# Score tiles kept in PSUM, a router on unnormalised tokens, and earlier expert panels in a two-layer float32 transformer kernel

## What is computed

```python
# layer 1 (x: 256 x 1024)
z = rms_norm(x) @ w_in                 # q, c_kv, q_idx, k_idx, w_idx, g_attn, x_rnn, g_rnn, merge
s_idx = sum_j relu(q_idx[j] @ layer_norm(k_idx).T) * w_idx[j]      # 8 index heads
keep  = top 64 keys of each token by s_idx, causal
o     = softmax(q_lat[h] @ c_kv.T - slope[h] * dist, over keep) @ c_kv   # 16 heads
y_a   = (o @ w_uv * silu(g_attn)) @ w_attn_proj
u     = causal_depthwise_conv(x_rnn)   # 4 taps
a     = exp(-8 * sigmoid(u @ w_a) * softplus(-lam))
h     = scan(h = a * h + sqrt(1 - a*a) * sigmoid(u @ w_x) * u)
x1    = x + (g_a * y_a + g_r * ((h * silu(g_rnn)) @ w_rnn_proj)) @ w_out
# layer 2: 8 MoBA heads and 8 MLA heads, gated and projected, then
x2    = rms(x1) + mixed2 @ w_out_2
hf    = rms_norm(x2)                   # ffn_norm gain
group = argmax(hf @ w_rg); the two best of its 8 experts by hf @ w_re   # 32 experts, width 256
out   = rms_norm(x2 + sum of weight * down(silu(hf @ gate) * (hf @ up)))
```

## Time and profile before

| | |
|---|---|
| median of 3 runs | 746.95 us (746.90 to 748.19) |
| the profiled execution | 748.94 us, span 747.1 us |
| PE busy | 666.2 us (89%) |
| DVE, ACT, POOL busy | 388.1, 333.6, 392.8 us |
| HBM read | 179.71 MB |
| transfer rate, 40 slices of 18.7 us | 421 GB/s in slices 27 and 28, 264 in slice 29, 415 to 423 in slices 30 to 39; 89 to 206 GB/s in slices 3 to 25 |
| mean granted clock of PE | 0.978 |

### The profile page before, as it was taken

One profiled execution on the slowest core, in us unless ns is written; L12 is line 12 of the kernel. 1 busy time (PEld: TensorE's weight loads), 2 busy tenths in 40 slices (PEclk: granted clock), 3 DMA queues, 4 the chain that ended last, 5 costly groups with the idle time before them and its releaser, 6 DMA issues.

```text
span 747.1 us, 13776 instructions
## 1 busy us (share of the span) xinstructions
PE 666.2 (89%) x5578; PEld 554.3 (74%) x5578; DVE 388.1 (52%) x664; ACT 333.6 (45%) x611; POOL 392.8 (53%) x284
## 2 busy tenths in 40 slices
PE   2999989989999999989999999998899997777754
PEld 2999879879989999988879998995654543343321
DVE  5899963599995247976855554624311110010002
ACT  7456657855653457554358665342212111111102
POOL 3789647687879989797798556970000000000000
PEclk9899999999999999999999999999999999999997
DMA  9735323433434554543454333799799999999992
GB/s 323 289 125 206 123 89 139 150 132 121 162 121 169 188 201 169 170 144 139 148 191 169 114 114 131 308 421 421 264 423 418 421 421 421 422 420 422 421 415 81
DMA packets 26129, 181.68 MB, mean 243 GB/s; under 512 B 2896, under 2 KB 3152, under 8 KB 4688
## 3 DMA queue, kind: packets, MB, share of 16 engines
q1 hardware_dynamic: 26064, 180.77, 63.2%
HBM read 179.71 MB, written 1.05 MB: 242 GB/s over the span
## 4 chain that ended last, share of the span: by engine, by line
PE 56%; DVE 19%; DMA 12%; issue 4%; ACT 4%; POOL 2%; SPq 2%; ACTq 0%; DVEq 0%
PE D L449 30%; PE L L880 5%; DVE big L1401 4%; DMA xT<-w_expert_dram 4%; DMA hT<-w_expert_dram 4%; DMA big<-w_expert_dram 4%; PE L L860 3%; PE QB L910 3%; DVE small L1401 2%; POOL ring_r L1384 2%; PE D L489 2%; PE D L917 2%; PE L L606 1%; SPq L388 1%; DVE big_r L1420 1%
## 5 line engine op out<-in xcount | busy, mean ns | idle before, releaser
L1384 POOL TENSOR_TENSOR ring_r<-ring,ring_r 128x512 fp32r<-128x512 f32 x280 | 392.6, 1437 | 108.6 <-ACT ring_r L1000 108.5
L449 PE MATMUL D<-scr_r,ring_r 128*128 128x256 f32 x1104 | 213.1, 289 | 0.7 <-DVE big L1401 0.7
L1000 ACT ACTIVATE ring_r<-ring 128x1024 fp32r<-128x1024 f32 x140 | 146.2, 1053 | 79.8 <-PE D L449 70.2
L449 PEld LDWEIGHTS D<-scr_r,ring_r 128*128 128x128 f32 x1104 | 175.3, 191 | 3.4 <-issue 2.1
L449 PE MATMUL D<-hT_r,ring_r 128*128 128x256 f32 x552 | 156.1, 283 | 0.0
L449 PE MATMUL D<-big_r,ring_r 128*128 128x256 f32 x1110 | 140.2, 287 | 4.4 <-POOL ring_r L1384 4.3
L449 PEld LDWEIGHTS D<-big_r,ring_r 128*128 128x128 f32 x1110 | 136.7, 195 | 6.7 <-POOL ring_r L1384 3.9
L449 PEld LDWEIGHTS D<-hT_r,ring_r 128*128 128x128 f32 x552 | 105.7, 192 | 1.2 <-issue 1.0
L1401 DVE SCALAR_TENSOR_TENSOR th<-th,L 64x256 f32<-64x256 f32 x32 | 13.4, 418 | 179.4 <-ACT th L1315 178.9
L1315 ACT ACTIVATE th<-L 64x256 f32<-64x256 f32 x16 | 6.0, 378 | 85.1 <-PE L L880 85.1
L860 PEld LDWEIGHTS L<-cst,big 128*128 128x128 f32 x256 | 29.8, 191 | 12.3 <-issue 12.3
(11 more groups left out here) (339 smaller groups left out, 1005.7 us busy)
## 6 DMA issues: line engine op xcount, KB each, us to landing
ring<-w_dense_dram SPq DMA_DIRECT2D x69, 1024.0 KB, 5.0
big<-w_expert_dram SPq DMA_DIRECT2D x40, 1024.0 KB, 24.9
ring<-w_expert_dram SPq DMA_DIRECT2D x30, 1024.0 KB, 26.5
wu<-w_expert_dram SPq DMA_DIRECT2D x6, 1024.0 KB, 24.6
attn<-w_expert_dram SPq DMA_DIRECT2D x5, 1024.0 KB, 20.2
scr<-w_expert_dram SPq DMA_DIRECT2D x5, 1024.0 KB, 27.0
hT<-w_expert_dram SPq DMA_DIRECT2D x5, 1024.0 KB, 27.3
xT<-w_expert_dram SPq DMA_DIRECT2D x5, 1024.0 KB, 27.6
```

The source lines that it names most:

```text
L449: last = mm(out_, r32(w[i][ws]), r32(x[j][xs_]), start=start and m == 0, stop=stop and m == 2)
L1000: A_(r32(hi_unit(j)), dense_unit(j), ACT.Copy).then_inc(hi_ready, 1)
L1384: last = g.tensor_tensor(r32(w), w, r32(h).bitcast(F32), ALU.subtract)
```

## The change

In the order of the program:

- x is loaded from ACT's queue, the first panel from SP's; ACT rounds unit 1 before it squares x; small steps of the softplus stand earlier on DVE.
- Index relus stay in their PSUM banks, and DVE adds from there. The norm of the latent stands behind the mask. The convolution's partial sums live in banks QB, UB, L0, L1. `rg_gates` waits for all eight chunks of it.
- Scores, biased scores and exponentials stay in L0 and L1; `normalise` goes from PSUM to `E`. `score_pair` waits for the probabilities of the pair before. Head outputs are gated and split straight from their banks.
- The decays go in smaller pieces, their squares behind `exps(4)`, the root ahead of a side gate.
- The router uses unnormalised x2 with the gain folded into its weights: 16 small matmuls with tokens as rows, three quarters of them between out2 units, and the squares are summed by 8 one-column matmuls. The root and the reciprocal are 128x2. `htok` is copied with that scale out of the accumulators. The second gather has a bank of its own, and DVE stages both.
- `wide_ring` has `scr` and `hT` as slots 1 and 2, and SP issues the first three panels among the last dense ones.
- The last pair's down panels hold column halves, its combine goes in quarters, the combine before it goes between the halves of gate_up, the root's table is loaded early, and the output is scaled by DVE and ACT and stored from both queues.

```diff
-        wide_ring = [wu[:], attn[:, 0:2 * UNIT], big[:, 4 * K:6 * K], ...
+        wide_ring = [wu[:], scr.rearrange("p c t -> p (c t)"), hT.rearrange("p c t -> p (c t)"), attn[:, 0:2 * UNIT],
...
+        CB = [QB, UB, L0, L1]
# SP
-                sp_.dma_start(xT[:, 4 * h:4 * h + 4, :], x_t[:, 4 * h * T:4 * (h + 1) * T].rearrange(
-                    "p (c t) -> p c t", c=4)).then_inc(s_in[f"x{h}"], 16)
...
+            dense(left.pop(0))
+            dense(left.pop(0))
+            sp_.wait_ge(unit_done, UNIT0["omoba"])
             expert(0)
             expert(1)
             dense(left.pop(0))
             expert(2)
+            dense(left.pop(0))
+            sp_.wait_ge(o_mm, H1 + 2 * H2)
             expert(3)
+            expert(4)
...
+            for q, units in ((10, 134), (11, 136), (12, 138), (13, 138), (14, 140), (15, 140), (16, 140), (17, 140)):
...
+            sp_.wait_ge(x2_in, 4)
             expert(18)
# PE
-                        pe.wait_ge(idx_relu, j - 2)
+                        pe.wait_ge(idx_acc, j - 2)
...
-                pe.wait_ge(conv_done, c + 1)
-                pe.wait_ge(idx_relu, IDXH)
+                pe.wait_ge(conv_done, 8)
...
-                pe.wait_ge(biased, a) if a else pe.wait_ge(gates, 8)
+                pe.wait_ge(probs, a) if a else pe.wait_ge(gates, 8)
...
+            def route(i):
+
+                kept(pe, "out2", i)
...
+                for c in (2 * i, 2 * i + 1):
+                    for tt in range(NT):
+                        mm(OB[:, tt * 64:tt * 64 + NG + NE], xT[:, c, tt * P:(tt + 1) * P], wrt[:, c, :],
+                           start=(c + tt == 0), stop=(c == DC - 1), skip_group_check=True)
+
+            def sum_tokens(c0):
+
+                for c in (c0, c0 + 1):
+                    for tt in range(NT):
+                        last = mm(OB[:, P + tt:P + tt + 1], x1_sq[:, c, tt * P:(tt + 1) * P], ones[:, 0:1],
+                                  start=False, stop=(c == DC - 1), skip_group_check=True)
+                return last
+
             chunk_pair("out2", (m2_hi, tg2), "m2")
             for c in range(2, 8):
                 chunk("out2", c, (m2_hi, tg2))
...
+                if c in (3, 5, 7):
+                    route(c // 2 - 1)
+
+            pe.wait_ge(folded, 3)
+            sum_tokens(0)
+            route(3)
+            pe.wait_ge(sq, SQ0[N_FFN] + 4)
+            sum_tokens(6).then_inc(ssq, 1)
...
                 gate_up_half(p, 0, x).then_inc(panel_used, 2)
+                pe.wait_ge(xe_ready, 2 * (p // 2) + 2)
+                if p + 1 == PAIRS:
+                    combine(p - 1)
                 gate_up_half(p, 1, x).then_inc(gu_done, 1)
# ACT
+            advance(2)
             squares(N_X, x_in)
-            advance(2)
...
+                if i == 2:
+                    act.wait_ge(idx_acc, IDXH)
...
-                    last = A_(u[:, c, :], bank[:, m * T:(m + 1) * T], ACT.Identity, bias=V("conv_b", c),
+                    last = A_(CB[i][:, m * T:(m + 1) * T], bank[:, m * T:(m + 1) * T], ACT.Identity,
...
-                    A_(scores_in[:, j % 4, :], IB[j % 4][:, 0:CAUSAL], ACT.Relu).then_inc(idx_relu, 1)
+                    A_(IB[j % 4][:, 0:CAUSAL], IB[j % 4][:, 0:CAUSAL], ACT.Relu).then_inc(idx_relu, 1)
...
+            A_(rt[:, 850:852], OB[:, P:P + 2], ACT.Sqrt, bias=sp[:, 9, 0:1], scale=1.0 / D).then_inc(rooted, 1)
...
+                act.wait_ge(x2_in, n + 1)
+                A_(htok[:, tt, h * 512:(h + 1) * 512], ACC[tt][h][:, :], ACT.Copy,
+                   scale=rt[:, 848 + tt:849 + tt]).then_inc(htok_ready, 1)
# DVE
-            dve.wait_ge(rel["dve"], 1)
-            norm(N_CKV, lambda c: zc[:, 0, :], lambda c: cT, "kv_norm_gain")
-
...
             v.tensor_tensor(Dm, score, C("dist", CAUSAL), ALU.add).then_inc(mask_ready, 1)
 
+            dve.wait_ge(rel["dve"], 1)
+            norm(N_CKV, lambda c: zc[:, 0, :], lambda c: cT, "kv_norm_gain")
+
...
+                taps = CB[c // 2][:, (c % 2) * T:(c % 2 + 1) * T]
                 for t in (2, 1, 0):
-                    ins = stt(u[:, c, :], xr[:, c, 1 + t:1 + t + T], V("conv_w", t * 8 + c), u[:, c, :],
+                    ins = stt(taps if t else u[:, c, :], xr[:, c, 1 + t:1 + t + T], V("conv_w", t * 8 + c), taps,
...
-                sa = S[:, a % 2, :]
+                sa = LB[a % 2][:, 0:CAUSAL]
...
-                    last = v.tensor_scalar(E[:, a % 2, c0:c0 + n], E[:, a % 2, c0:c0 + n],
+                    last = v.tensor_scalar(E[:, a % 2, c0:c0 + n], LB[a % 2][:, c0:c0 + n],
```

More of the change, by code:

```diff
@@ L235, in build @@
         y_out = at(small, 2 * K, NT, D)
-        rlogT = at(small, 4 * K, T)
+        x1_sq = at(small, 2 * K, DC, T)
         ye = at(small, 4 * K, 2, 512)
@@ L425, in _ @@
                 expert(q)
[L427 to L430, removed]
+            for tt in range(NT):
+                sp_.wait_ge(out_scaled, tt + 1)
+                sp_.dma_start(out[:, (2 * tt + 1) * 512:(2 * tt + 2) * 512], y_out[:, tt, 512:1024]).then_inc(stored, 16)
             sp_.wait_ge(stored, 16 * 2 * NT)
@@ L904, in down @@
             def down(p, b):
-                w = [expert_panel(pe, 6 * p + 4 + e).rearrange("p (k h f) -> p k h f", k=2, h=2) for e in range(2)]
+                w = [expert_panel(pe, 6 * p + 4 + h).rearrange("p (e k f) -> p e k f", e=2, k=2) for h in range(2)]
                 for k in range(2):
@@ L945, in _ @@
                         pe.wait_ge(ye_ready, p)
-                    down(p, p % 2).then_inc(y_mm, 1)
                     if p + 1 < PAIRS:
+                        down(p, p % 2).then_inc(y_mm, 1)
                         sw_transposes(p + 1, release=2)
-                pe.wait_ge(ye_ready, PAIRS)
-                pe.wait_ge(swt_ready, PAIRS)
-                for tt in range(NT):
-                    add_experts((PAIRS - 1) % 2, tt, True).then_inc(x2_ready, 1)
+                last_down(0)
+                last_down(1)
+                last_combine(0)
+                last_combine(1)
             with pe.Else():
@@ L1030, in x_in @@
                 return xT[:, c:c + w, :]
+            for h in range(2):
+                act.dma_start(xT[:, 4 * h:4 * h + 4, :], x_t[:, 4 * h * T:4 * (h + 1) * T].rearrange(
+                    "p (c t) -> p c t", c=4)).then_inc(s_in[f"x{h}"], 16)
             act.wait_ge(sp_step, 2)
@@ L1176, in _ @@
             keys_in(0)
+            decays(0, 2)
             for m in range(H1 // 2 + 1):
@@ L1182, in _ @@
                     exps(2 * m)
+                    if m == 2:
+                        decay_squares()
                     advance(ahead + 1)
@@ L1190, in _ @@
                     keys_in(m + 1)
+                if m < 2:
+                    decays(2 + 3 * m, 4 + 2 * m)
+                if m == 2:
+                    act.wait_ge(m_ready, 1)
+                    A_(lru_m, lru_m, ACT.Sqrt).then_inc(rt_m, 1)
                 if m < H1 // 2:
@@ L1193, in _ @@
                 if m < 2:
-                    decays(4 * m, 4 * m + 4)
-                if m == 2:
-                    act.wait_ge(m_ready, 1)
-                    A_(lru_m, lru_m, ACT.Sqrt).then_inc(rt_m, 1)
+                    decays(4 + 2 * m, 5 + 3 * m)
             for i in range(4):
@@ L1770, in _ @@
             cnt, rank, wv, part = rt[:, 416:448], pair(560, NE), pair(624, NE), pair(688, NE)
-            dve.wait_ge(padz, 2)
-            dve.wait_ge(rlog_mm, 1)
-            v.tensor_scalar(rlogT[0:NG + NE, :], QB[0:NG + NE, 0:T], V("b_router")[0:NG + NE], None,
-                            ALU.add).then_inc(rlog_kept, 1)
-            dve.wait_ge(rlog, 1)
-            step(v.tensor_copy(gpad[:, :, 0:NG], lg[:, :, 0:NG]))
+            gpad = lgs[:, :, NE:NE + 8]
+            dve.wait_ge(rooted, N_FFN + 1)
+            v.reciprocal(rt[:, 848:850], rt[:, 850:852]).then_inc(rinvd, 1)
+            dve.wait_ge(rinvd, N_FFN + 1)
+            for tt in range(NT):
+                last = stt(lgs[:, tt, 0:NE + NG], OB[:, tt * 64:tt * 64 + NE + NG], rt[:, 848 + tt:849 + tt],
+                           V("b_router", 0, NE + NG), ALU.mult, ALU.add)
+            step(last)
             for tt in range(NT):
```

344 lines of the change are left out of this document (180 added, 164 removed).

## The result

The changed kernel takes 741.66 us (median of 4 runs, 740.54 to 744.46) against 746.92 us: ratio 0.9931, 95% interval 0.9905 to 0.9957. A second set of six runs beside the experiments gave 740.87 us and 0.9922 (0.9897 to 0.9947). So it is faster by some 5.5 us, not by 12.9: the sign was right, the size well short, and 741 to 742 lies just outside the range. I read two profiles of it, the first with a span of 742.7 us (its execution took 744.46), the second with 739.2 us; the kernel before has 747.1.

A forecast was written before the change was run, and what follows sets the result against it. Bound by the dense part, the stretch to the first panel release, and the expert panel stream with its tail. Terms 2.7 - 12.0 - 3.6 = -12.9 us against 746.95 gave 734 us, range 726 to 741.

The forecast's parts named there:

- wait at q and the spell behind it: Before the first q unit PE waits for the latent, now normalised behind the mask: +7.9 us, then half-rate clock, +1.7.
- convolution: 24 DVE adds fall from 0.88 to about 0.5 us, the wait for all eight chunks costs nothing: -2 us.
- first attention: PE's waits for ACT, 2.8 + 1.6 us, go with smaller ACT pieces and a faster DVE: -4.4 us.
- units 54 to 88 (POOL relief): POOL, less held up by DVE, gives PE's units a little earlier: -1 us (0 to -2).
- second layer's start, and its first scores: No cost: no term for the start; `score_pair`'s stricter wait has 1.5 us of cover in the second attention, so nothing.
- dense part: Everything up to the last dense unit, 508.11 us before: its terms sum to +2.7 us.
- last dense unit to release: From the last out2 unit to the first freed panel slot: 27.1 us becomes 15.1, -12.0 us.
- tail: From the last gate_up to the span's end, 20.2 us before: -3.6 us (-2 to -5).
- the residual's 3.6 us lie beside the routing now: Between last dense unit and release, PE's residual matmuls run beside DVE's routing, so they add no time.
- from 7 us to 2: The hole in the expert panel transfers before the first release shrinks from 7 us to 2.
- the stream takes the gain back: Rival, chance 0.10: the three early panels don't get ahead, so only the 7 us hole can be lost; 739 us.
- PSUM gives DVE nothing: Rival, chance 0.12: DVE gains nothing from PSUM, the wait at q is 14 us; 744.5 us, or 739 for half.

The follow-up runs named there:

- experiment 1: Changed kernel with PE's wait for the normalised latent moved from before the first q unit to behind the third; 732.02 us, ratio 0.9793.
- experiment 2: Changed kernel with DVE's latent norm back ahead of the index search, PE's wait still before the first q unit; 733.48 us, ratio 0.981.
- experiment 4: Changed kernel with the old order of wide slots and panel issues, apart from two slots freed earlier by the new router; 741.86 us, ratio 0.9934.
- Experiment 8: Changed kernel with DVE's 128x2048 product `lru(1)` moved one round earlier, into an idle stretch of DVE; 737.04 us, ratio 0.9851.
- experiment 3: Changed kernel with the gain multiplication of the router's weights moved to just ahead of the second attention; 740.23 us, ratio 0.9899.
- experiment 10: Changed kernel with PE's latent wait behind the third q unit, the router's gain multiplication late and the 128x2048 product a round earlier; 727.87 us, ratio 0.9752.
- experiment 6: Changed kernel with PE's latent wait behind the third q unit, and the convolution's partial sums in SBUF again; 739.83 us, ratio 0.9872.
- experiment 7: Changed kernel with moved latent wait, late gain multiplication, rank matmuls before the residual's last quarter, gate_up(0)'s first half before the second gather; 732.59 us, ratio 0.9787.

## Why the prediction was wrong in size

By its own steps, against the second profile, whose span is 7.9 us under that of before (12.9 were predicted):

| step | predicted | measured |
|---|---|---|
| start | -1.2 | -1.2 |
| wait at q and the spell behind it | +7.9, +1.7 | +7.0, +2.6 |
| convolution | -2 | -1.7 |
| first attention | -4.4 | -3.3 |
| units 54 to 88 (POOL relief) | -1 | -0.8 |
| second layer's start, and its first scores | 0 | +1.1, +0.5 |
| router matmuls between out2 units | +1.7 | +1.5 |
| **dense part** | **+2.7** | **+5.7** |
| last dense unit to release | -12.0 | -11.2 |
| release to last half of gate_up | 0 | +0.9 |
| tail | -3.6 | -3.4 |

**Right:** the wait at q, its place, price and spell, and experiments 1 and 2 confirm it as the cause. That wait and spell come to 9.6 us exactly as forecast is partly luck: the latent was ready 2.4 us and PE there 1.1 us earlier than counted, which makes the wait 0.9 us shorter with the hand-over, and the spell cost 0.9 more. The wait for all eight chunks of the convolution had its cover. The release and the tail were right where PE ran at full clock: 15.3 us in experiment 4, from the end of the last matmul as the prediction counts it, against 15.1, and a tail of 16.8 us.

**Wrong, and the largest part (3.0 of the 5.0 us): the dense part.** First, "The ACT waits, 2.8 + 1.6" for -4.4 took it that a wait goes when its named releaser gets faster. I hadn't asked what was late next: DVE's 2.5 us product. Experiment 8 shows that the attention had 5.7 us to give. That is 1.1 us. Second, the second layer was put at nothing up to the router, and it lost 1.6. Of this 1.1 us are DVE's two products in POOL's company (experiment 3). The gain multiplication, which I had read in the change and costed nowhere, had its cover; the step that failed is that DVE's chain there stood in no term of the sum, though POOL now works beside it at other times. The other 0.5 is the stricter wait of `score_pair`: "1.5 us of cover, so nothing" was read in one pair, and another pair, at 402.7, waited 0.4 us for `normalise`, as the same pair did in all these kernels, with unit 110 some 0.5 us later. The rest is small: convolution 0.3 and POOL 0.2 less than counted. And POOL's -0.8 is luck: 0.1 of it lies between units 54 and 84, the rest at units 85 and 86, where the kernel before had its half-rate spell and the changed kernel had none behind an idle place of 2.5 us.

**Wrong: "the residual's 3.6 us lie beside the routing now".** They did at full clock only. 5.0 to 6.5 us, most of them at the lower clock, made PE late next, 0.7 to 2.3 us. I had priced a spell behind an idle place, but none where PE is busy.

**Half right: the hole goes "from 7 us to 2".** By the DMA shares it was 5.5 us before, not 7 (0.81, 0.04 and 0.33 of 3 us each from 528 to 537), and it went to 3.9 in the first profile and to 2.4 in the second. 0.9 us of the release's shift got lost between the release and the last half of gate_up; what took it is open.

The rival "the stream takes the gain back" came nearest in time (739), for another reason: it put the loss into the stream, and experiments 1, 8 and 10 show that the stream passed on what the dense part gave. "PSUM gives DVE nothing" falls with experiment 6.

## What to carry to other kernels

A wait belongs in front of the first instruction that reads the data, not at the head of the stage: here one line was worth 9 to 10 us, more than the whole change brought. When a wait is to go because its releaser gets faster, look up what stands in front of that releaser on each engine; it is the next to be late. Before a small difference between two kernels is put down to an edit, look whether kernels without that edit show it too: here 1.0 us at units 88 to 108 came and went in kernels that are the same in that stage. And a saving that lies under another wait shows only once that wait is gone, so edits are judged together.

## What the hardware showed unexpectedly

- The granted clock fell from 2.4 to 1.2 GHz with PE busy all the time, some 3 us into 3.8 us of matmuls with 36 and 1 columns (513.7 to 517.6), and for different lengths in executions of one kernel. In nine of the thirteen profiles with these matmuls it fell there, in those of experiments 4, 6, 7 and 8 it did not; what decides it is open.
- A DVE product over 128x256 with both inputs in SBUF took 1.00 us beside POOL and 0.48 when POOL rested; the mask step over 128x384 1.53 and 0.56. Two such products further on took 1.91 us beside POOL and 0.88 behind it, and the second layer's start came 1.0 us later with the slow pair.
